# Moving an expert stage's token gathers and result scatters from TensorE to indirect DMA

## What is computed

```python
gates = sum(one_hot(top2 indices) * softmax(top2 logits))
for e in range(8):                       # wg[e], wu[e]: 1024x1408, wd[e]: 1408x1024, f32
    y = y + gates[..., e:e+1] * ((silu(x @ wg[e]) * (x @ wu[e])) @ wd[e])
h = h + y
```

## Time and profile before

| | before |
|---|---|
| median of three runs | 977.94 us |
| the profiled execution | 977.73 us, span 975.9 us |
| PE busy | 926.8 us (95%) |
| DVE / ACT / POOL busy | 722.3 / 524.6 / 122.1 us |
| moved from and to HBM | 220.31 / 3.99 MB, 230 GB/s over the span |

### The profile page before, as it was taken

How to read it: one execution, slowest core, us unless ns; L and a number is a source line. 1 busy time by engine, 2 the same in 40 slices (tenths; PEclk the granted TensorE clock), 3 DMA queues, 4 the chain that set the end, 5 groups by cost and what they waited for, 6 DMA issues and landing times.

```text
span 975.9 us, 14777 instructions
## 1 busy us (share of the span) xinstructions
PE 926.8 (95%) x6085; PEld 809.1 (83%) x6085; DVE 722.3 (74%) x877; ACT 524.6 (54%) x579; POOL 122.1 (13%) x158
## 2 busy tenths in 40 slices
PE   4999989999999997999989999999999999999976
PEld 3999789999999997998867777777777777777775
DVE  3786475655555676885569888898898979898965
ACT  5322354443445354322438877777668667777642
POOL 3337121100110013424210000000000000000001
PEclk9999899999999998998989999999999999999978
DMA  9973355746674657524317986999789988989601
GB/s 320 310 222 104 77 173 167 192 139 216 186 184 137 207 173 194 169 95 110 126 60 264 402 333 244 395 367 345 285 318 357 338 322 319 364 341 380 233 3 45
DMA packets 119798, 224.85 MB, mean 230 GB/s; under 512 B 4882, under 2 KB 88978, under 8 KB 119584
## 3 DMA queue, kind: packets, MB, share of 16 engines
q1 hardware_dynamic: 117664, 216.63, 63.2%
q0 software_dynamic: 2064, 7.23, 3.1%
HBM read 220.31 MB, written 3.99 MB: 230 GB/s over the span
## 4 chain that ended last, share of the span: by engine, by line
PE 82%; DVE 9%; ACT 5%; issue 2%; DMA 1%; POOL 1%; SPq 0%; DVEq 0%; ACTq 0%; POOLq 0%
PE bank L683 13%; PE bank L684 12%; PE bank L685 12%; PE bank L961 7%; PE bank L959 7%; PE bank L960 7%; DVE wlo L1364 5%; PE bank L981 4%; PE bank L983 4%; PE bank L982 4%; ACT whi L1131 2%; PE bank L903 1%; PE bank L904 1%; PE bank L934 1%; PE bank L849 1%
## 5 line engine op out<-in xcount | busy, mean ns | idle before, releaser
L1364 DVE TENSOR_TENSOR wlo<-raw,whi 128x1408 fp32r<-128x1408 f32 (+2 forms) x294 | 480.2, 1653 | 120.4 <-ACT whi L1131 119.9
L1131 ACT ACTIVATE whi<-raw 128x1408 fp32r<-128x1408 f32 (+2 forms) x294 | 398.7, 1381 | 188.2 <-PE bank L685 101.9
L683 PE MATMUL bank<-xh,whi 128*128 128x264 f32 x672 | 197.1, 293 | 19.9 <-DVE xl L1375 11.0
L684 PE MATMUL bank<-xl,whi 128*128 128x264 f32 x672 | 193.7, 288 | 0.0
L685 PE MATMUL bank<-xh,wlo 128*128 128x264 f32 x672 | 193.4, 288 | 0.0
L683 PEld LDWEIGHTS bank<-xh,whi 128*128 128x128 f32 x672 | 130.0, 193 | 21.8 <-DVE wlo L1364 20.3
L959 PE MATMUL bank<-whi,xeh 128*96 128x512 f32 (+1 forms) x384 | 143.7, 374 | 0.6 <-DVE hid L1652 0.6
L961 PE MATMUL bank<-whi,xel 128*96 128x512 f32 (+1 forms) x384 | 143.9, 375 | 0.0
L960 PE MATMUL bank<-wlo,xeh 128*96 128x512 f32 (+1 forms) x384 | 143.5, 374 | 0.0
L684 PEld LDWEIGHTS bank<-xl,whi 128*128 128x128 f32 x672 | 130.2, 194 | 0.4
L685 PEld LDWEIGHTS bank<-xh,wlo 128*128 128x128 f32 x672 | 129.3, 192 | 0.0
(11 more groups left out here) (231 smaller groups left out, 1347.3 us busy)
## 6 DMA issues: line engine op xcount, KB each, us to landing
raw<-in_moe_w_gate SPq DMA_DIRECT2D x32, 1408.0 KB, 6.8
raw<-in_moe_w_up SPq DMA_DIRECT2D x32, 1408.0 KB, 7.6
raw<-in_moe_w_down SPq DMA_DIRECT2D x40, 1024.0 KB, 6.3
raw<-in_w_in SPq DMA_DIRECT2D x20, 1024.0 KB, 7.5
raw<-in_ffn_w_down SPq DMA_DIRECT2D x16, 704.0 KB, 4.9
raw<-in_ffn_w_gate SPq DMA_DIRECT2D x10, 1024.0 KB, 5.4
raw<-in_ffn_w_up SPq DMA_DIRECT2D x10, 1024.0 KB, 5.5
raw<-in_w_o SPq DMA_DIRECT2D x8, 1024.0 KB, 6.5
```

The source lines that it names most:

```text
L683: pe.matmul(out, w_hi, x_hi, start=start, stop=False)
L684: pe.matmul(out, w_hi, x_lo, start=False, stop=False)
L1131: act.activation(unit_hi(u), unit_raw(u), ACT.Copy).then_inc(hi_ready, 1)
L1364: dve.tensor_tensor(unit_lo(u), unit_raw(u), unit_hi(u).bitcast(F32), ALU.subtract).then_inc(lo_ready, 1)
```

## The change

Tokens of pairs 1 to 3 are fetched from DRAM. POOL adds xth and xtl to xt (in place, 128 x 3072) once the first pair's gathers are done, writes it to a DRAM tensor `tokens` in three transfers, and for each later pair fetches 96 rows of 4 KB per expert by an indirect DMA to xg[0] and xg[1]. PE transposes them with four transposes per step. The first pair is gathered as before.

Results of experts 0 to 5 are evicted by ACT alone, in f32, to ys[0] or ys[1]. POOL adds them to rows of a DRAM tensor `summed` by an indirect DMA with an add, one expert after another; `summed` is cleared by a transfer of zeros ahead of the stage. Empty slots go to spare rows behind the 264. After expert 5, POOL brings the 264 rows back in three transfers to xt, and PE transposes them during gu7 (three transposes per chunk), from where DVE adds them to h. DVE works out the two row lists in slot_values, which moves from the d phases to gu1, gu3 and gu5 (RG_AFTER). Experts 6 and 7 are scattered as before.

```diff
+RG_AFTER = 10
-SCATTER_AFTER = 1
+SCATTER_AFTER = 7
...
+            def gathered_columns(p, g, b):
+                a, half = divmod(g, 2)
+                if half == 0:
+                    pe.wait_ge(xg_in[a], 16 * p)
+                for c in range(4):
+                    mm = pe.transpose(b[:, c * CAP:(c + 1) * CAP], xg[a][0:CAP, (4 * half + c) * P:(4 * half + c + 1) * P],
+                                      ident[0:CAP, 0:CAP])
+                mm.then_inc(ga_full, 1)
+
+            def summed_columns(m):
+                b = bank[6 + m % 2]
+                if m == 0:
+                    pe.wait_ge(sum_in, 48)
+                if m < 2:
+                    pe.wait_ge(y_hi, 2 * BY_DMA)
+                else:
+                    pe.wait_ge(h_added, m - 1)
+                for j, w in BLK:
+                    mm = pe.transpose(b[:, j * P:j * P + w], xt[0:w, j, m * P:(m + 1) * P], ident[0:w, 0:w])
+                mm.then_inc(sc_full, 1)
...
-                            if e >= 2 and 0 <= i - SCATTER_AFTER < DC:
-                                scatter(e - 2, i - SCATTER_AFTER)
+                            if e % 2 and e < NE - 1 and i == RG_AFTER:
...
+                                pe.wait_ge(pick_ready, (e + 1) // 2 + 1)
+                                slot_values((e + 1) // 2, bank[6])
+                            if e == BY_DMA + 1 and 0 <= i - SCATTER_AFTER < DC:
+                                summed_columns(i - SCATTER_AFTER)
...
-                                gather(p, g, bank[3 + g % 3])
-                                if g == 3:
-                                    pe.wait_ge(xe_lo, STEPS_IN * p + 2)
-                                    slot_values(p, bank[4])
+                                gathered_columns(p, g, bank[3 + g % 3])
...
             def y_out_hi(e):
                 act.wait_ge(unit_used, U_FF[1] + MOE_AT["d", e] + DOWN)
+                if 2 <= e <= BY_DMA:
+                    act.wait_ge(sum_added, 16 * (BY_DMA if e == BY_DMA else e - 1))
+                dst = ys[e % 2] if e < BY_DMA else yh
...
             def slot_values(p, b):
...
+                token = rgs[0:CAP, p % 2, :, VALS - 1]
+                if p >= 2:
+                    dve.wait_ge(sum_added, 16 * (2 * p - 2))
+                if p:
+                    dve.tensor_scalar(from_row[0:CAP, p % 2, :], token, -1.0, 0.0, ALU.add, ALU.max).then_inc(rows_ready, 1)
...
             def y_out_lo(e):
+                if e < BY_DMA:
+                    return
...
+            def gather(p):
+                for a in range(2):
+                    pool.wait_ge(rows_ready, (1, 3, 5)[p - 1] + 1)
+                    if p == 1:
+                        pool.wait_ge(ga_full, STEPS_IN)
+                    else:
+                        pool.wait_ge(ga_full, STEPS_IN * (p - 1) + 2 * a + 2)
+                    pool.indirect_dma_start(xg[a][0:CAP, :], None, tokens[:, :],
+                                            bass.IndirectOffsetOnAxis(from_row[0:CAP, p % 2, a:a + 1], 0)).then_inc(xg_in[a], 16)
+
+            def add_rows(e):
+                pool.wait_ge(rows_ready, (1, 3, 5)[e // 2])
+                pool.wait_ge(y_hi, 2 * e + 2)
+                pool.wait_ge(sum_added if e else sum_clear, 16 * max(e, 1))
+                pool.indirect_dma_start(summed[:, :], bass.IndirectOffsetOnAxis(to_row[0:CAP, e // 2 % 2, e % 2:e % 2 + 1], 0),
+                                        ys[e % 2][0:CAP, :], None, compute_op=ALU.add).then_inc(sum_added, 16)
+
+            def experts():
+                pool.wait_ge(ga_full, STEPS_IN)
+                pool.tensor_tensor(xt[:, :, :], xth[:, :, :].bitcast(F32), xtl[:, :, :].bitcast(F32), ALU.add).then_inc(xt_free, 1)
+                pool.wait_ge(xt_free, 1)
+                for j, w in BLK:
+                    pool.dma_start(tokens[j * P:j * P + w, :], xt[0:w, j, :]).then_inc(xt_out, 16)
+                pool.wait_ge(xt_out, 48)
+                for p in range(1, PAIRS):
+                    gather(p)
+                    for e in (2 * p - 2, 2 * p - 1):
+                        add_rows(e)
+                pool.wait_ge(sum_added, 16 * BY_DMA)
+                for j, w in BLK:
+                    pool.dma_start(xt[0:w, j, :], summed[j * P:j * P + w, :]).then_inc(sum_in, 16)
...
                     pool.dma_start(trow[:, :], t["trow"]).then_inc(trow_in, 16)
+                    pool.dma_start(summed[0:T, :], t["zeros"]).then_inc(sum_clear, 16)
                 square_sum(4 if l else 1)
```

More of the change, by code:

```diff
@@ L461, in program @@
         xtl = moe("xtl", [P, 3, D], F32R)
+        xg = [place(f"xg{a}", [P, D], F32, arena + 4 * a * D) for a in range(2)]
+        xt = place("xt", [P, 3, D], F32, arena + 4 * 3 * D)
         r = {n: moe("r_" + n, [P, 3, NE]) for n in
@@ L475, in program @@
         flag = moe("flag", [1, 1], I32)
+        empty = moe("empty", [P, 2])
+        spare = moe("spare", [P, 1])
+        from_row, to_row = moe("from_row", [P, 2, 2], I32), moe("to_row", [P, 2, 2], I32)
         pickT = moe("pickT", [P, T], F32R)
@@ L490, in program @@
         yl = place("yl", [P, D], F32R, dead + 4 * D)
+        ys = [place(f"ys{a}", [P, D], F32, dead + 4 * a * D) for a in range(2)]
         owt = place("owt", [P, 2, EC * P], F32, arena)
@@ L581, in unit_hi @@
             return whi[:, HIGH_AT[u]:HIGH_AT[u] + COLS[u]]
+        tokens = nc.dram_tensor("tokens", [T, D], F32, kind="Internal").ap()
+        summed = nc.dram_tensor("summed", [SPARE, D], F32, kind="Internal").ap()
         def y_bank(e):
@@ L942, in gate_up @@
                 pe.wait_ge(lo_ready, u + 1)
[L943 to L944 removed]
+                if e == 0 and i % 4 == 0:
+                    pe.wait_ge(xe_lo, k // 2 + 1)
+                elif e % 2 == 0 and i % 8 == 0:
+                    pe.wait_ge(xe_lo, STEPS_IN * p + k // 4 + 1)
                 H, L = unit_hi(u), unit_lo(u)
@@ L970, in down @@
                     pe.wait_ge(hl_ready, 3)
+                elif i == 0 and e <= BY_DMA - 1:
+                    pe.wait_ge(y_hi, 2 * e)
+                    pe.wait_ge(rg_ready, min((e + 3) // 2, PAIRS))
                 elif i == 0 and e < NE - 1:
-                    pe.wait_ge(h_added, DC * e)
+                    pe.wait_ge(h_added, DC)
                 elif i == 0:
@@ L1633, in slot_values @@
                                   AX_X, ALU.add).then_inc(rg_ready, 1)
+                dve.wait_ge(rg_ready, p + 1)
                 if p + 1 < PAIRS:
                     picks(p + 1)
+                token = rgs[0:CAP, p % 2, :, VALS - 1]
[3 more added lines that the diff above has]
+                    dve.tensor_scalar(from_row[0:CAP, p % 2, :], token, -1.0, 0.0, ALU.add, ALU.max).then_inc(rows_ready, 1)
+                else:
+                    step(dve.tensor_scalar(spare[0:CAP, :], C("tokid", CAP)[:, 0:1], float(T), None, ALU.add))
+                if p < BY_DMA // 2:
+                    step(dve.scalar_tensor_tensor(out=empty[0:CAP, :], in0=token, scalar=0.0,
+                                                  in1=spare[0:CAP, :].to_broadcast([CAP, 2]), op0=ALU.is_equal, op1=ALU.mult))
+                    dve.scalar_tensor_tensor(out=to_row[0:CAP, p % 2, :], in0=token, scalar=-1.0, in1=empty[0:CAP, :],
+                                             op0=ALU.add, op1=ALU.add).then_inc(rows_ready, 1)
             def hid_lo(e, s, b):
@@ L1692, in experts @@
                                 hid_lo(0, s, bank[6 + s % 2])
-                            if e >= 2 and 0 <= i - SCATTER_AFTER < DC:
-                                scattered(e - 2, i - SCATTER_AFTER)
+                            if e % 2 and e < NE - 1 and i == RG_AFTER:
+                                slot_values((e + 1) // 2, bank[6])
+                            if e == BY_DMA + 1 and 0 <= i - SCATTER_AFTER < DC:
+                                scattered(BY_DMA - 1, i - SCATTER_AFTER)
                             if i == GU_UNITS - 1:
@@ L1966 @@
         "trow": token_row(),
+        "zeros": np.zeros((T, D), np.float32),
     }
```

54 lines of the change are left out of this document (34 added, 20 removed).

## The result

The changed kernel takes 970.39 us (970.04 to 970.99, 4 runs) against 977.60 us (976.48 to 977.95, 4 runs): ratio 0.9929, 95% interval 0.9912 to 0.9946, so it is 0.7% faster, clear of no change and small. The forecast was 963.6 us. The direction was right and half of the gain is missing. The profiled execution took 970.41 us, its span is 968.5.

The account below looks back on a forecast made before the run. PE was taken as the bound of the expert stage; -21.3 + 1.0 + 4.7 + 1.0 + 0.5 = -14.1 us on the profiled 977.7 gave 963.6 us, with a range from 955.5 to 977.

Parts of the forecast that it names:

- What PE loses: Expert stage: gathers -11.8 us, scatters in gu2 to gu6 -10.4, gu7's transposes in place of scatters +0.9; together -21.3 us.
- A column: gu7: three transposes for one chunk of the sums cost PE 0.35 us, eight sets +0.9 us net of the scatters replaced.
- DVE's and ACT's lead: Even d phases: PE and DVE come close to equal, so DVE's usual lead is not won; +1.0 us (0 to 4).
- POOL's addition: gu0: addition of 5.7 us holds DVE's splits, PE stands 3.0 us, lower clock costs 1.7; +4.7 us (0 to 8).
- The fetch of tokens: From gu1, gu3, gu5, unit 10: row list, issue and landing take 8.3 of 12.4 us, so hidden; 0 us.
- DMA time: Whole expert stage: 7 to 9.4 MB more traffic fits beside the weights; +0.5 us for bursts (0 to 4).
- The sums brought back: After d5: last add and three transfers take 16.3 us, PE wants the first column after 15.3; +1.0 us (0 to 14).
- The third: Rival: DMAs land as late as under a loaded POOL queue, fetches and sums late, 996 us at 13 us landing; chance 0.17.
- L: Landing time of each indirect DMA in the third rival's formula for lateness of fetches and sums; it decides from L = 10.
- The second rival: Each POOL DMA waits for a DVE split, 1.6 us; four in a row before gu7's columns; 972 us; chance 0.17.
- the fourth: Rival: feed becomes the bound, DVE's lead used up after even d phases, some 4 us x 3; 975 us; chance 0.08.
- The signs set for being wrong: PE waits for xg or over 8 us in gu7, weight transfers end PE's waits, or indirect DMAs land after over 10 us.

## Why the prediction was right in sign and wrong in size

- *What PE loses.* Right, and too low. Gathers and scatters together gave 24.8 us in d0 to d5 against 11.8 + 10.4 forecast, although the slot values that moved cost 0.45 us in each odd gu phase (in gu3 the unit behind which they stand and the next start 669.07 - 666.71 = 2.36 us apart instead of 1.91). The even d phases came out at 18.0, the number named.
- *A column.* Forecast 0.35 us, measured 0.54 to 0.55: eight cost 4.3 to 4.4, not 2.8. The narrow transpose and the changeover, for which no row of their own stood in the prediction, make up the difference. PE loses about 2.0 us in gu7 by it, not 0.9.
- *DVE's and ACT's lead.* The 1.0 us did not appear: between d0 and d5 PE has three waits for DVE, 0.8 us together, and the even d phases have the length named.
- *POOL's addition.* The mechanism, the place and the clock behind it were as said. The size was 7.1 us in place of 4.7: the addition took 7.92 us, not 5.7, of which 1.2 can be a split that ran already (518.38 + 3.15 = 521.53) and 1.0 stays open; PE stood 4.06, not 3.0; the lower clock cost 2.7, not 1.7. Another 0.4 is the slot values in gu1.
- *The fetch of tokens.* Hidden, as said, but with hardly a margin. Counted from the first issue, the budget was 10.0 us (576.42 to the transposes at 586.46), not some 11, and issue and landing took 9.5, not 1.2 + 5.5. In most of the kernels that followed PE waited 0.4 to 1.7 us for these rows.
- *DMA time.* The 0.5 us did not appear: no wait of PE in the stage is ended by a weight transfer.
- ***The sums brought back.*** This is the step that failed. The prediction took 1.0 + 5.5 us for issue and landing of the last addition and 0.6 + 7.7 for the sums; measured were 9.8 (840.71 to 850.49) and 10.9 (850.49 to the columns). With 2.2 instead of 1.5 ahead of the first issue the chain came to 22.9 us instead of 16.3, the wait to 7.48 instead of 1.0, and the clock behind it cost 1.8 for which nothing stood in the sum. With the columns gu7 lost 11.2 us where 1.9 were forecast. The 5.5 us were chosen from 128 KB that landed in 2.4 and 132 KB that landed in 5.8, for 384 KB "beside the weights". The DMA share of the kernel before tells these rows apart (the stretches of the three landings; the last two numbers are the share and GB/s):

```profile
22.60:35.70 13.10, 12.88 (x92) 12.71 (x93) 10.38 (x9) 6.04 (x5) 6.29 (x12) 0.87 1.08 293
447.50:451.00 3.50, 3.50 (x31) 3.50 (x30) 2.89 (x3) 0.42 (x1) 3.07 (x4) 1.00 0.15 37
479.00:485.00 6.00, 6.00 (x52) 6.00 (x51) 3.66 (x6) 2.54 (x3) 1.65 (x3) 1.00 0.97 354
```

The 2.4 stands for engines that were nearly idle. The two rows from stretches as full as the stage's 1.02 are the 5.8, for a third of the bytes of a fetch, and the 13.1, which the prediction used only as the far bound.
- *The rivals.* The third had the right mechanism. With L = 9.5 its formula gives 3.1 + 9.5 + 11.5 - 15.3 = 8.8 us for the sums, 1.7 for the clock and nothing for the fetches, close to what came. It was priced from L = 10 up only, in the main as a case that ends slower; just below that it is what happened. What the prediction held against it was a misreading: the 1 MB that took 13.1 us did not stand behind six POOL DMAs, it was the first that POOL issued (at 22.61, the five others from 24.48 on). The second rival was right in a small part beside DVE's added work (0.8 to 0.9 us for an indirect DMA) and not in gu7's chain, the fourth not at all in the changed kernel.
- *The sum.* Measured against forecast, the terms miss by -2.6 (PE's work), +1.1 (columns), -1.0 (lead), +2.4 (POOL's addition), +8.3 (the sums with their clock) and -0.5 us (DMA time), +7.7 in all (-14.1 + 7.7 = -6.4, where the stage measures 6.5 less). The sums alone are more than that, and it is luck that the rest nearly cancels. The signs set for being wrong did not catch it: the wait of 7.48 us stayed just under the 8 named, and of the indirect DMAs a single one passed the 10, with 10.2 us from the start of its issue.

What stays open: the 1.1 us by which the stage began earlier, the 1.0 us of POOL's addition, why the first addition of rows landed sooner than the others, and how the 9.2 us of an addition of rows divide into reading, adding and writing.

## What to carry to other kernels

Take the landing time of a new transfer from rows of a stretch as full as the one in which it will run: here 512 KB took 3.7 us on idle DMA engines and 8.6 beside weight transfers, and a chain of two such transfers decided the gain. When work is moved to DMA, ask first where its result is needed and put the use as late as the data flow lets you; moving the same eight columns one phase on was worth 8 us. By the traces of this case, an addition with both operands in SBUF is cheaper on a nearly full DVE, in pieces of 0.67 us, than on an idle POOL that shuts DVE out; the difference, 1.0 us against POOL's pieces, is too small for the times to prove.

## What was not expected of the hardware

- The exclusion of DVE and POOL hits even the smallest operation: one of 3 elements took 6.32 us instead of 0.15 beside a POOL addition. It works the other way round too, over several instructions: a POOL piece of 512 elements took 6.52 us instead of 1.3 to 2.0 beside DVE splits of 1.6 us each.
- Indirect DMAs cost POOL 0.99 to 3.5 us of issue each where a plain one of this change costs 0.54 to 0.58; the first of a pair 2.92, the second 1.23 us in d0's fetch.
- An addition of rows in DRAM landed in 5.3 us on idle engines where a fetch of as many rows took 4.0; beside the weights the two were alike (9.2 and 9.5). All four count from the start of the issue.
